# The last projection of a transformer pair in two token halves, from plain fp32 weights kept in the gather ring

## The chip, the cores and the metric

One core of a Trainium2 chip. The metric is the device time of one execution in microseconds, the median of the runs. Engines: TensorE (PE), VectorE (DVE), ScalarE (ACT), GpSimd (POOL), and SyncE (SP), which only issues DMAs here.

## What is computed

A two-layer transformer (feed-forward, gated linear attention, stick-breaking attention) is followed by one hybrid block. Only the end of that block matters here: 256 tokens, width 1024, fp32.

```python
mixed = sigmoid(g_s) * y_s + sigmoid(g_m) * (y_mlstm @ w_ml_out)
h = h + mixed @ w_out                        # the last projection
xn = rmsnorm(h, norm2_g)
q = (xn @ w_q).reshape(T, 8, 2, 128)         # 8 heads, two halves each
s = einsum('thid,hikd->thik', q, keys)       # 128 sub-keys for each half
sv, si = top_k(s, 16)                        # then the 16 best of 16 x 16 sums
gate = softmax(cs)                           # over the 16 experts chosen, ids eidx
act = gelu(einsum('td,thkd->thk', xn, u_tab[eidx]))
h = h + einsum('thk,thkd->td', gate * act, v_tab[eidx])
return rmsnorm(h, final_norm_g)
```

Each token reads 8 x 16 rows of a table that holds a row of `u` and one of `v` side by side (2048 fp32). With the tokens in two halves of 128 (one token per partition) that makes 2 x 8 x 16 = 256 gathers, each of 128 rows of 8 KB, 1 MiB.

## The kernel before

**Weights.** All weights but the last come as 512 KB packets (128 x 1024 fp32) that SyncE loads in order into six raw slots (`weights_in`, L511). ScalarE copies a packet to the high part (`refill`, L216), GpSimd subtracts it for the low part (L553), and TensorE multiplies high and low parts as fp32r. The sixteen packets of the query weights `w_q` are used as they came, in plain fp32: six in the raw slots, eight over the split buffers, one over `h`, and the last again in a raw slot (`query_slot`, L161; L534 to L542).

**The last two projections.** `mix_out` (L2305) multiplies `w_ml_out` (eight packets) and combines each of the eight 128-wide output chunks with the gates in PSUM (`total`, L2365), then splits the sums into `xs` (L2353, L2374). `add_projection` (L872) multiplies the eight packets of `w_out` for all 256 tokens: for each of eight chunks `mm_both` issues two matmuls, L208 (128x512: high weights by both parts of the input) and L209 (128x256). VectorE adds the residual (L927, L929), ScalarE copies the sum to `x` (L897) and writes it times the norm's gain to `over_xs` (L905).

**`peer` (L2389).** The first two query packets run for tokens 0 to 127 (`half(n, 0)`, L2565), then their key scores (`half_scores(0)`, L2572); VectorE's `first_route` (L2744) takes the best expert of head 0 at once and the next seven a little later, so that the first eight gathers can start. TensorE meanwhile runs the tokens 128 to 255 of the same packets, the sums of squares (`columns_pe`, L402), the transposes of the first half (`turn`, L2591), packets 2 and 3 for all tokens (`tile`, L2553) with their scores (L2583), and `begin(0)`, which puts the residual into the accumulators (L2598, L2600).

Then come 256 slots in order, one for each gather (n = 0 to 255; first half first; 16 per head):

- GpSimd issues gather n (L2659) into `ring[n % 8]`. For n of 8 or more it waits for `px_free`, the end of slot n - 8 on TensorE. Only eight gathers can be under way.
- VectorE multiplies and sums the `u` part with the token's hidden vector (`dot`, L2794) and between dots runs two steps of the routing of the next head.
- ScalarE makes gelu (L2474), weight (L2478) and a diagonal matrix (L2482), four of which exist.
- TensorE adds diagonal by `v` part in two 128x512 matmuls (L2608).

The other twelve query packets are put between slots by a table written out by hand, `PE_TILE_AT` (L47): a `tile` ahead of slots 2, 8, 16, 23 and so on up to 82, and the scores five slots behind every second one. The rings: six slots in the arena, one over `small_all`, one over `k.sq`; gather 7, into the last, waits for the norm's columns and for `pr_sqdone` (L2654).

The engines' queues are in order, so what stands ahead of slot 0 on TensorE or ScalarE delays it.

Of the kernel before, what the change touches and what calls it, by code (L numbers as in the profile page):

```python
# [15 lines left out]
P = 128  # L16
# [31 lines left out]
PE_EVICT_LAG = 3  # L48
PE_SCORES_LAG = 5
# [166 lines left out]
def refill(k, act, n, i=None):  # L216
# [3 lines left out]
    if i is None:  # L220
        if m >= AT["peer_q"]:
# [289 lines left out]
def weights_in(k, block, wstream):  # L511
# [3 lines left out]
    def _(sp):  # L515
# [8 lines left out]
        p0, last = AT["peer_q"], AT["peer_q"] + RAW  # L524
        full = last // RAW
# [6 lines left out]
        for n in range(full * RAW, last):  # L532
            sp.wait_ge(k.lo_done, n - RAW + 1)
            sp.dma_start(k.raw[:, n % RAW, :], wstream[n]).then_inc(k.landed[n % RAW], 16)  # L534
        for j in range(2 * SPLIT):

            if j % 2 == 0:
                sp.wait_ge(k.tile_done, p0 - SPLIT + j // 2 + 1)
            sp.dma_start(query_slot(k, RAW + j), wstream[last + j]).then_inc(k.query_in[j], 16)
        sp.dma_start(query_slot(k, 14), wstream[p0 + 14]).then_inc(k.query_in[8], 16)  # L540
        sp.wait_ge(k.tile_done, p0 + 1)
        sp.dma_start(query_slot(k, 15), wstream[p0 + 15]).then_inc(k.query_in[9], 16)  # L542
# [1762 lines left out]
def mix_out(k, block, ins):  # L2305
# [3 lines left out]
    sums, frees = k.mixes, k.frees  # L2309
    k.mixes += DC  # L2310
    k.frees += DC - 1
    late = 5
# [3 lines left out]
    def _(pe):  # L2316
# [22 lines left out]
        for n in range(3, 8):  # L2339
            wait_packet(k, pe, packet + n)  # L2340
            mm_packet(k, pe, packet + n, ps[:, bank[n], 0:SEQ], leaves=k.xs_free if n == 7 else None).then_inc(k.tile_done, 1)

    @block.scalar
    def _(act):
# [3 lines left out]
        def high(c):  # L2348

            if c < DC - 1:  # L2350
                act.wait_ge(k.xs_free, frees + c + 1)
            act.wait_ge(k.mix_sum, c + 1)
            act.activation(k.xs[:, 0, c, 0:SEQ], ps[:, bank[c], 0:SEQ], ACT.Copy).then_inc(k.mix_high, 1)  # L2353

        for n in range(6):
            refill(k, act, packet + n)
        for c in range(7):
            high(c)
        refill(k, act, packet + 6)
        high(7)  # L2360
        refill(k, act, packet + 7)

    @block.vector
    def _(dve):
        def total(n):  # L2365
            dve.wait_ge(k.tile_done, packet + n + 1)
            b = ps[:, bank[n], 0:SEQ]
            k.dve(dve.tensor_tensor(b, b, k.sig[:, 16 + n, :], ALU.mult))
            k.dve.settle(dve)
            dve.tensor_tensor(b, b, k.sig[:, 8 + n, :], ALU.add).then_inc(k.mix_sum, 1)  # L2370

        def rest(c):
            dve.wait_ge(k.mix_high, c + 1)
            dve.tensor_tensor(k.xs[:, 1, c, 0:SEQ], ps[:, bank[c], 0:SEQ], k.xs[:, 0, c, 0:SEQ].bitcast(F32), ALU.subtract  # L2374
                              ).then_inc(k.mix_ready, 1)

        dve.wait_ge(k.sig_made, 3)
        for n in range(7):
            total(n)
        for c in range(late):  # L2380
            rest(c)
        total(7)
        for c in range(late, DC):
            rest(c)

    add_projection(k, block, AT["w_out"], k.mix_ready, k.mixes, tuple(range(DC)), GAIN["norm2"], by_chunk=True, first=5, whole=True)


def peer(k, block, gain, ins, out):  # L2389
# [5 lines left out]
    k.norms += 1  # L2395
    k.early += 1
    k.columns += 1
# [34 lines left out]

    @block.scalar
    def _(act):
        late_refill(k, act)
        act.wait_ge(k.x_copied, k.copies)

        def square(i):
            act.activation(k.sq[:, 2 * i:2 * i + 2, 0:SEQ] if i else sum_bank(k, 7), x[:, 2 * i:2 * i + 2, :], ACT.Square
                           ).then_inc(k.sq_ready, 1)  # L2440

        def half(n, t):

# [664 lines left out]
```

## Time and profile before

| | |
|---|---|
| median of 3 runs | 1936.19 us (1935.8 to 1937.76) |
| the profiled execution's own time | 1936.39 us |
| its span, first to last instruction | 1934.6 us |
| mean granted TensorE clock | 0.995 |
| HBM read over the span | 484.10 MB |
| software-descriptor DMA queue (the gathers) | 268.45 MB, 36864 packets |
| first query product starts, `w_out` done | 1265.14 us |
| first slot's matmul starts | 1287.20 us |

How to read it: the page divides the span into 40 slices of 48 us; the gathers fill the last third. The timeline lists instructions of one engine in order, like ones merged, each with its start, its duration, and in brackets how long the engine had been idle and what released it. A plain fp32 matmul leaves two records (x2), an fp32r one leaves one.

### The profile page before, as it was taken

The page shows a single profiled execution, that of the slowest core. Times are in us where ns is not written, and L with a number is a line of the kernel's source. Part 1 is how long each engine was busy: PE and PEld are TensorE (multiplying, and loading weights), DVE is VectorE, ACT ScalarE, POOL GpSimd, SP SyncE. Part 2 cuts the span into 40 slices and gives each one's busy share as a digit, 9 for nine tenths or more (in the row PEclk, how much of TensorE's full clock was granted, in tenths as well). Part 3 has the DMA queues.
Part 4 walks back from the last instruction along what each step waited for, and adds up shares of the span by engine and source line. Part 5 has one row for each costly group of instructions (what it writes and reads, how often), then busy time and mean ns, then how long its engine had stood idle before and what let it go on. Part 6 is the DMA issues. An engine that isn't in the chain of part 4 may idle for free.

```text
span 1934.6 us, 29255 instructions
## 1 busy us (share of the span) xinstructions
PE 1804.0 (93%) x9861; PEld 1366.0 (71%) x9864; DVE 1145.7 (59%) x2481; ACT 949.7 (49%) x1757; POOL 1224.1 (63%) x708
## 2 busy tenths in 40 slices
PE   8999999999999999999999999999999877778777
PEld 7999888999999998789998878875544322222222
DVE  5444555444644466754457775576677666777664
ACT  5444646444544465654448445454444444444443
POOL 8888665888788877388887962534444343433441
PEclk9999999999999999999999999999999999999999
DMA  7666443666566555266654341599999999999996
GB/s 269 186 186 190 152 144 125 197 189 185 169 196 188 185 167 166 80 188 188 187 184 140 122 152 55 154 389 421 421 421 421 421 421 418 421 422 419 422 420 283
DMA packets 98426, 486.76 MB, mean 252 GB/s; under 512 B 11920, under 2 KB 12944, under 8 KB 65312
## 3 DMA queue, kind: packets, MB, share of 16 engines
q1 hardware_dynamic: 60304, 213.20, 35.6%
q0 software_dynamic: 36864, 268.45, 33.4%
q10 hardware_dynamic: 1168, 3.96, 0.6%
q8 instruction: 50, 0.82, 0.2%
q14 instruction: 40, 0.33, 0.0%
HBM read 484.10 MB, written 1.05 MB: 251 GB/s over the span
## 4 chain that ended last, share of the span: by engine, by line
PE 68%; DMA 16%; DVE 5%; ACT 5%; POOL 4%; issue 2%; DVEq 0%; ACTq 0%; POOLq 0%
DMA arena<-uv_tab,arena 16%; PE ps L827 16%; PE ps L2608 10%; PE ps L178 8%; PE ps L179 8%; PE ps L180 8%; PE ps L825 7%; PE ps L208 2%; POOL split L1824 2%; PE ps L2553 2%; DVE arena L2794 1%; ACT arena L2482 1%; PE ps L209 1%; PE ps L830 1%; POOL arena L1828 1%
## 5 line engine op out<-in xcount | busy, mean ns | idle before, releaser
L553 POOL TENSOR_TENSOR split<-raw,split 128x1024 fp32r<-128x1024 f32 x358 | 859.0, 2407 | 292.6 <-ACT split L228 287.9
L228 ACT ACTIVATE split<-raw 128x1024 fp32r<-128x1024 f32 x382 | 404.7, 1063 | 494.7 <-PE ps L180 263.0
L2608 PE MATMUL ps<-arena 128*128 128x512 f32 x1024 | 494.2, 617 | 101.7 <-ACT arena L2482 101.4
L2659 POOL DMA_INDIRECT arena<-uv_tab,arena x256 | 268.4, 1049 | 383.8 <-PE ps L2608 350.9
L827 PE MATMUL ps<-xs,split 128*128 128x512 f32 x1344 | 470.6, 393 | 0.0
L2608 PEld LDWEIGHTS ps<-arena 128*128 128x128 f32 x1024 | 181.9, 191 | 400.6 <-ACT arena L2482 248.2
L825 PE MATMUL ps<-xs,split 128*128 128x256 f32 x1176 | 328.5, 279 | 0.0
L827 PEld LDWEIGHTS ps<-xs,split 128*128 128x128 f32 x1344 | 247.0, 188 | 43.5
L825 PEld LDWEIGHTS ps<-xs,split 128*128 128x128 f32 x1176 | 221.1, 188 | 6.9
L2794 DVE CUSTOM_DVE_ANT_0 arena<-arena,raw 128x1024 f32<-128x1024 f32 x128 | 156.8, 1225 | 103.9 <-DMA arena<-uv_tab,arena 103.2
L2794 DVE CUSTOM_DVE_ANT_0 arena<-arena 128x1024 f32<-128x1024 f32 x128 | 156.9, 1226 | 91.4 <-DMA arena<-uv_tab,arena 90.6
L783 DVE TENSOR_TENSOR ps<-ps,arena 128x512 f32<-128x512 f32 x84 | 58.7, 699 | 250.4 <-PE ps L827 250.4
L2474 ACT ACTIVATE arena<-arena 128x1 f32<-128x1 f32 x256 | 51.8, 202 | 310.9 <-DVE arena L2794 310.7
L178 PE MATMUL ps<-h,split 128*128 128x256 f32 x704 | 199.0, 283 | 0.1
L180 PE MATMUL ps<-h,split 128*128 128x256 f32 x704 | 199.0, 283 | 0.0
L179 PE MATMUL ps<-h,split 128*128 128x256 f32 x704 | 198.9, 282 | 0.0
L178 PE MATMUL ps<-xs,split 128*128 128x256 f32 (+1 forms) x608 | 175.7, 289 | 4.4 <-POOL split L1824 2.8
L179 PE MATMUL ps<-xs,split 128*128 128x256 f32 (+1 forms) x608 | 172.2, 283 | 0.0
L180 PE MATMUL ps<-xs,split 128*128 128x256 f32 (+1 forms) x608 | 172.0, 283 | 0.0
L179 PEld LDWEIGHTS ps<-h,split 128*128 128x128 f32 x704 | 134.5, 191 | 3.4
L178 PEld LDWEIGHTS ps<-h,split 128*128 128x128 f32 x704 | 134.2, 191 | 0.4 <-issue 0.4
L180 PEld LDWEIGHTS ps<-h,split 128*128 128x128 f32 x704 | 134.4, 191 | 0.0
(424 smaller groups left out, 2742.2 us busy)
## 6 DMA issues: line engine op xcount, KB each, us to landing
raw<-wstream SPq DMA_DIRECT2D x393, 512.0 KB, 3.5
over_split<-wstream SPq DMA_DIRECT2D x8, 512.0 KB, 6.6
arena<-uv_tab,arena POOLq DMA_INDIRECT x256, 15.1
arena<-small SPq DMA_DIRECT2D x1, 1195.0 KB
arena<-xT SPq DMA_DIRECT2D x1, 1024.0 KB, 6.2
arena<-keys ACTq DMA_DIRECT2D x1, 1024.0 KB, 7.9
arena<-rows ACTq DMA_DIRECT2D x1, 512.0 KB, 4.5
over_h<-wstream SPq DMA_DIRECT2D x1, 512.0 KB, 8.4
```

The lines of the kernel that those rows point to most:

```text
L178: pe.matmul(out, w_hi, x_hi, start=start, stop=False, **kw)
L179: pe.matmul(out, w_hi, x_lo, start=False, stop=False, **kw)
L180: return pe.matmul(out, w_lo, x_hi, start=False, stop=stop, **kw)
L228: act.activation(parts_of(k, m)[0], raw_slot(k, m), ACT.Copy).then_inc(k.hi_done, 1)
L553: pool.tensor_tensor(lo, raw_slot(k, n), hi.bitcast(F32), ALU.subtract).then_inc(k.lo_done, 1)
L783: dve.tensor_tensor(both(4 + b), both(4 + b), rstd, ALU.mult).then_inc(k.gate_scaled, 1)
L825: pe.matmul(k.ps[:, bank, 0:SEQ], lo[:, c, :], k.xs[:, 0, c, 0:SEQ], start=False, stop=False, skip_group_check=True)
L827: last = pe.matmul(both(bank), hi[:, c, :], k.xs[:, :, c, 0:SEQ], start=(c == 0), stop=(c == DC - 1), skip_group_check=True)
L2474: k.act(act.activation(acts[:, b, s:s + 1], dots[:, b, s:s + 1], ACT.Gelu_apprx_tanh))
L2608: last = pe.matmul(ps[:, banks[t][0] + i, :], diag[:, n % 4, :], ring[n % NS][:, D + i * 512:D + (i + 1) * 512], start=False, stop=ends, s ...
L2659: pool.indirect_dma_start(ring[n % NS], None, ins["uv_tab"], bass.IndirectOffsetOnAxis(ap=ids[:, b, s:s + 1], axis=0)).then_inc(k.px_in[n ...
L2794: dve.tensor_tensor_reduce(u, u, ht[t], 1.0, 0.0, ALU.mult, ALU.add, dots[:, b, s:s + 1]).then_inc(k.px_dot, 1)
```

## The change

The last projection leaves `add_projection`. The mixed sums stay in `sig` as plain fp32 and aren't split. The eight packets of `w_out` are loaded unsplit into an arena range, `w_last`, over which four of the eight ring slots lie (ring numbers 4 to 7); a ring slot there may be gathered into once two of the packets are done with. Each packet is multiplied in plain fp32 for tokens 0 to 127 first (`last_part(n, 0)`); the products for tokens 128 to 255 (`last_part(n, 1)`) are put among the first tokens' query products, scores and transposes. The query products of packets 0 to 3 now all run in token halves, the second half only after `begin(0)`. The norm's column for the second half is made at slots 14 to 20. The query packets are loaded eight packets earlier, and packet 15 goes over the low half of `xs`. Gather 7 no longer waits for the norm; gathers 4 to 7 wait for second-half products 2, 4, 6 and 8.

```diff
+PE_NORM_AT = 18
 def weights_in(k, block, wstream):
...
-        for n in range(full * RAW, last):
-            sp.wait_ge(k.lo_done, n - RAW + 1)
-            sp.dma_start(k.raw[:, n % RAW, :], wstream[n]).then_inc(k.landed[n % RAW], 16)
+        sp.wait_ge(k.mix_ready, 3 * DC)
+        for j in range(DC):
+            sp.dma_start(k.w_last[:, j, :], wstream[w0 + j]).then_inc(k.last_in[j // 2], 16)
+        sp.dma_start(query_slot(k, 14), wstream[p0 + 14]).then_inc(k.query_in[4], 16)
+        for n in range(RAW):
+            sp.wait_ge(k.lo_done, w0 + n - RAW + 1)
+            sp.dma_start(query_slot(k, n), wstream[p0 + n]).then_inc(k.landed[n % RAW], 16)
         for j in range(2 * SPLIT):
             if j % 2 == 0:
-                sp.wait_ge(k.tile_done, p0 - SPLIT + j // 2 + 1)
+                sp.wait_ge(k.tile_done, w0 - SPLIT + j // 2 + 1)
...
 def mix_out(k, block, ins):
+        def total(n, lo=0, hi=SEQ):
+            b, s = ps[:, bank[n], lo:hi], k.sig[:, 8 + n, lo:hi]
+            k.dve(dve.tensor_tensor(b, b, k.sig[:, 16 + n, lo:hi], ALU.mult))
+            k.dve.settle(dve)
+            dve.tensor_tensor(s, b, s, ALU.add).then_inc(k.mix_ready, 1)
...
-    add_projection(k, block, AT["w_out"], k.mix_ready, k.mixes, tuple(range(DC)), GAIN["norm2"], by_chunk=True, first=5, whole=True)
 def peer(k, block, gain, ins, out):
...
+        def last_part(n, t, lo=0, hi=DC):
+            if t == 0 and lo == 0:
+                pe.wait_ge(k.last_in[n // 2], 32)
+                if n >= 2:
+                    pe.wait_ge(k.dve_emptied, emptied + n - 1)
+            if t and n % 4 == 0:
+                pe.wait_ge(k.dve_emptied, emptied + DC - 1 + n // 4)
             for c in range(lo, hi):
+                if n < 2 and t == 0:
+                    pe.wait_ge(k.mix_ready, sums + max(c, 5) + 1)
+                if n == 0 and t == 1 and c == DC - 1:
+                    pe.wait_ge(k.mix_ready, sums + DC + 1)
+                last = pe.matmul(area(n, t), k.w_last[:, n, c * P:(c + 1) * P], mixed[:, c, T[t]],
                                  start=(c == 0), stop=(c == DC - 1))
...
+        for n in range(2, DC):
+            last_part(n, 0)
         half(0, 0)
         half(1, 0)
-        half(0, 1, 0, 2)
-        pe.wait_ge(k.pr_q, 2)
+        last_part(0, 1)
         pe.wait_ge(k.keys_in, 16)
-        half_scores(0)
-        half(0, 1, 2, DC)
-        half(1, 1)
-        pe.wait_ge(k.sq_sum, r + 1)
-        columns_pe(k, pe, cq)
-        tiles.wait_emptied(pe, 1)
-        pe.wait_ge(k.pr_sc, 1)
-        half_scores(1)
+        half_scores(0, 0)
+        turn(0, 6)
+        half(2, 0)
+        half(3, 0)
+        last_part(1, 1)
+        columns(0)
+        last_part(2, 1)
         pe.wait_ge(k.col_rms, cq + 1)
-        turn(0, 6)
-        for n in range(2, PE_TILES_FIRST):
-            tile(n)
-            if n % 2:
-                scores(n // 2)
+        half_scores(1, 0)
+        for n in range(3, DC):
+            last_part(n, 1)
         pe.wait_ge(k.pr_ht, 1)
         begin(0)
+        half(0, 1)
+        half(1, 1)
+        half_scores(0, 1)
+        half(2, 1)
+        half(3, 1)
+        half_scores(1, 1)
         for n in range(SLOTS):
+            if n == PE_NORM_AT + 1:
+                pe.wait_ge(k.pr_sc, 6)
+                columns(1)
...
-            if n == NS - 1:
-                pool.wait_ge(k.col_rms, cq + 1)
-                pool.wait_ge(k.pr_sqdone, 1)
+            if NS // 2 <= n < NS:
+                pool.wait_ge(k.tile_done, w0 + 2 * (n - NS // 2) + 2)
...
+        def added(n, t):
+            dve.wait_ge(*((k.tile_done, w0 + (n | 3) + 1) if t else (k.last_half, n + 1)))
+            dve.tensor_tensor(x[:, n, T[t]], area(n, t), x[:, n, T[t]], ALU.add).then_inc(k.dve_emptied, 1)
...
         hidden(0, 6)
...
+        for n in range(DC):
+            added(n, 1)
         for g in range(GROUPS):
...
                 dot(g * PE_K + s)
+                if g * PE_K + s == PE_NORM_AT:
+                    squares(1, 1, 4)
+                if g * PE_K + s == PE_NORM_AT + 2:
+                    inverse(1)
```

ScalarE ahead of slot 0 now runs, in this order: `scaled(0, c)` (gain times x into `over_xs`) with three of the four squares, `half(0, 0)`, `half(1, 0)`, `half_scores(0, 0)`, the last square, the Sqrt table, `columns(0)`, `half(2, 0)`, `half(3, 0)`, `half_scores(1, 0)`, the first exponentials, `scaled(1, c)`, and the four halves and two scores of the second half. At slots 14 to 17 it runs `square(1, i)` and at slot 20 `columns(1)`.

## Rows read from the trace of the kernel before

**Rows 1.** The page, part 2: DMA throughput in 40 equal slices.

```profile
GB/s 269 186 186 190 152 144 125 197 189 185 169 196 188 185 167 166 80 188 188 187 184 140 122 152 55 154 389 421 421 421 421 421 421 418 421 422 419 422 420 283
```

**Rows 2.** Windows: us, busy of each engine, PEclk, DMA share, GB/s.

```profile
1220.00:1240.00 20.00, 19.46 (x165) 19.25 (x164) 9.58 (x22) 8.13 (x10) 11.60 (x5) 1.00 0.55 166
...
1260.00:1280.00 20.00, 20.00 (x141) 18.59 (x140) 12.33 (x52) 10.05 (x24) 4.33 (x5) 1.00 0.98 374
1280.00:1300.00 20.00, 18.61 (x75) 12.20 (x75) 19.31 (x58) 12.27 (x31) 8.78 (x9) 1.00 1.01 415
```

**Rows 3.** Timeline of VectorE, end of the mLSTM: start, us, operation.

```profile
1225.50 0.69 DVE L2132 TENSOR_TENSOR xs<-ps,xs 128x512 fp32r<-128x512 f32 x1 [0.74 <-ACT xs L1992]
```

**Rows 4.** Timeline of TensorE, first matmul of the projection.

```profile
1242.70 0.50 PE L208 MATMUL ps<-xs,split 128*128 128x512 f32 x1
```

**Rows 5.** Timeline of TensorE from the projection to the slots.

```profile
1265.14 4.38 PE L2565 MATMUL ps<-over_xs,raw 128*128 128x128 f32 x36
1269.44 0.71 PE L2572 MATMUL ps<-arena 128*128 128x128 f32 x4
1269.99 3.29 PE L2565 MATMUL ps<-over_xs,raw 128*128 128x128 f32 x28
1273.11 1.01 PE L402 MATMUL ps<-arena 128*128 128x1 f32 x8
...
1274.52 1.06 PE L2591 MATMUL ps<-arena 128*128 128x128 f32 x8
1275.41 7.07 PE L2553 MATMUL ps<-over_xs,raw 128*128 128x256 f32 x32
...
1284.38 1.95 PE L2600 MATMUL ps<-arena 128*128 128x128 f32 x16
1287.20 3.70 PE L2608 MATMUL ps<-arena 128*128 128x512 f32 x8 [0.87 <-ACT arena L2482]
1290.74 3.62 PE L2553 MATMUL ps<-over_xs,raw 128*128 128x256 f32 x16
1294.19 10.60 PE L2608 MATMUL ps<-arena 128*128 128x512 f32 x24
```

**Rows 6.** Timeline of ScalarE ahead of slot 0.

```profile
1284.15 0.66 ACT L2461 ACTIVATE arena<-ps 128x256 f32<-128x256 f32 x2 [1.25 <-PE ps L2583]
1284.83 1.28 ACT L2474 ACT_TABLE_LOAD   x1
...
1286.74 0.40 ACT L2482 ACTIVATE arena<-arena 128x128 f32<-128x128 f32 x1
```

**Rows 7.** Timeline of GpSimd: issues of gathers 0, 1, 8, 10, 16.

```profile
1272.70 1.15 POOL L2659 DMA_INDIRECT arena<-uv_tab,arena  x1 [14.57 <-DVE arena L2766]
1275.91 0.94 POOL L2659 DMA_INDIRECT arena<-uv_tab,arena  x1 [2.06 <-DVE arena L2716]
...
1289.96 0.94 POOL L2659 DMA_INDIRECT arena<-uv_tab,arena  x1 [4.48 <-PE ps L2608]
...
1296.34 0.94 POOL L2659 DMA_INDIRECT arena<-uv_tab,arena  x1 [3.96 <-PE ps L2608]
...
1310.73 1.91 POOL L2659 DMA_INDIRECT arena<-uv_tab,arena  x1 [4.19 <-PE ps L2608]
```

**Rows 8.** Tile view of one gather issue, number 1.

```profile
L2659 POOL DMA_INDIRECT arena<-uv_tab,arena x1: 939/939/939, 1275.9 to 1275.9; - x1
...
DMA to landing us min/median/max: 5.7/5.7/5.7
```

**Rows 9.** Timeline of VectorE: hidden vector; dots of slots 10, 16, 255.

```profile
1281.92 1.28 DVE L2673 SCALAR_TENSOR_TENSOR arena<-ps,arena 128x1024 f32<-128x1024 f32 x1
...
1305.74 1.23 DVE L2794 CUSTOM_DVE_ANT_0 arena<-arena 128x1024 f32<-128x1024 f32 x1 [0.91 <-DMA arena<-uv_tab,arena]
...
1320.54 1.23 DVE L2794 CUSTOM_DVE_ANT_0 arena<-arena 128x1024 f32<-128x1024 f32 x1 [1.25 <-DMA arena<-uv_tab,arena]
...
1924.71 1.23 DVE L2794 CUSTOM_DVE_ANT_0 arena<-arena,raw 128x1024 f32<-128x1024 f32 x1 [1.24 <-DMA arena<-uv_tab,arena]
```

More of the change, by code:

```diff
@@ L523, in _ @@
             sp.dma_start(dst, src).then_inc(k.small_in, 16)
-        p0, last = AT["peer_q"], AT["peer_q"] + RAW
-        full = last // RAW
+        w0, p0 = AT["w_out"], AT["peer_q"]
+        full = w0 // RAW
+        assert w0 % RAW == 0
         with sp.Fori(1, full) as i:
@@ L2308, in mix_out @@
     ps = k.ps
[L2309 to L2312, printed above, removed]
+    sums = k.mixes
+    k.mixes += DC + 1
     bank = (4, 2, 3, 5, 0, 1, 6, 7)
@@ L2346, in _ @@
         act.dma_start(k.peer_keys, ins["keys"]).then_inc(k.keys_in, 16)
[L2348 to L2355, printed above, removed]
[L2356 to L2361 removed]
+        for n in range(DC):
+            refill(k, act, packet + n)
     @block.vector
     def _(dve):
[L2365 to L2386 removed]
+        def total(n, lo=0, hi=SEQ):
[3 more added lines that the diff above has]
+            dve.tensor_tensor(s, b, s, ALU.add).then_inc(k.mix_ready, 1)
+        dve.wait_ge(k.sig_made, 3)
+        for n in range(DC):
+            dve.wait_ge(k.tile_done, packet + n + 1)
+            if n < DC - 1:
+                total(n)
+            else:
+                total(n, 0, P)
+                total(n, P, SEQ)
 def peer(k, block, gain, ins, out):
@@ L2394, in peer @@
     r, e0, cq = k.norms, k.early, k.columns
-    k.norms += 1
-    k.early += 1
-    k.columns += 1
+    w0 = AT["w_out"]
+    mixed = k.sig[:, DC:2 * DC, :]
+    sums, emptied = k.mixes - DC - 1, k.dve_tiles
+    T = (slice(0, P), slice(P, SEQ))
+    area = lambda n, t: ps[:, 2 + n // 4, P * (n % 4):P * (n % 4 + 1)] if t else ps[:, 2 + n % 2, 0:P]
     take = k.arena.take
@@ L2566, in half @@
                                  start=(c == 0), stop=(c == DC - 1))
             if hi == DC:
-                last.then_inc(k.tile_done if t else k.pr_half, 1)
-        def half_scores(t):
+                last.then_inc(k.tile_done if t else k.last_half, 1)
+        def half(n, t):
+            if t == 0:
+                query_landed(k, pe, n)
+            w = query_slot(k, n).rearrange("p (c m) -> p c m", c=DC)
+            for c in range(DC):
+                if n == 0:
+                    pe.wait_ge(k.xl_ready, DC * (e0 + t) + c + 1)
+                last = pe.matmul(half_at(n, t), w[:, c, :], k.over_xs[:, 0, c, T[t]], start=(c == 0), stop=(c == DC - 1))
+            last.then_inc(k.tile_done if t else k.pr_half, 1)
@@ L2573, in half_scores, with columns @@
                                  start=True, stop=True)
             last.then_inc(k.pr_s if t else k.pr_s0, 1)
+        def columns(t):
+            pe.wait_ge(k.sq_sum, r + t + 1)
+            for c in range(2):
+                last = pe.matmul(ps[:, 5 - t, 0:1], sq[:, c, :], k.ones[:, 0:1], start=(c == 0), stop=(c == 1))
+            last.then_inc(k.col_ss, 1)
         def scores(h):
             tiles.wait_emptied(pe, 2 * h + 1)
-            if h >= 2:
-                pe.wait_ge(k.pr_sc, 2 * (h - 1))
+            pe.wait_ge(k.pr_sc, max(2 * (h - 1), 4))
+            if h == 4:
+                pe.wait_ge(k.col_rms, cq + 2)
@@ L2664, in _, with squares @@
     def _(dve):
-        norm_low(k, dve, e0, x, gain)
-        sum_squares(k, dve, r, last=3)
+        def added(n, t):
+            dve.wait_ge(*((k.tile_done, w0 + (n | 3) + 1) if t else (k.last_half, n + 1)))
+            dve.tensor_tensor(x[:, n, T[t]], area(n, t), x[:, n, T[t]], ALU.add).then_inc(k.dve_emptied, 1)
+        def squares(t, first, last):
+            for i in range(first, last):
+                dve.wait_ge(k.sq_ready, 4 * (r + t) + i + 1)
+                step = dve.tensor_tensor(sq[:, 0:2, :], sq[:, 0:2, :], sq[:, 2 * i:2 * i + 2, :], ALU.add)
+                if i < 3:
+                    k.dve(step)
+                    k.dve.settle(dve)
+                else:
+                    step.then_inc(k.sq_sum, 1)
+        for n in range(DC):
+            added(n, 0)
+        squares(0, 1, 3)
         def hidden(t, first):
@@ L2815, in _ @@
             run(step)
+        for n in range(DC):
+            added(n, 1)
         for g in range(GROUPS):
```

157 lines of the change are left out of this document (93 added, 64 removed).

## The prediction

> **What bounds the kernel now.** I read the page's slices first. From the slice that begins near 1300 us to the last but one the DMA engines move 418 to 422 GB/s [rows 1]: the last third is a stream of 256 gathers of 1 MiB at the engines' full rate. The timeline of VectorE says the same: the dots of slots 10, 16 and 255 are released by their gather's landing [rows 9], and from dot 10 to dot 255 lie 618.97 us, 2.53 us for each. After dot 255 come a fixed 9.9 us to the end of the span. So the end is set by when the stream first runs without a gap, and the reader should ask of every edit: does gather 10 or 16 land earlier or later?
>
> What holds the stream's start? Gather 0 goes out at 1272.70 and the next from 1275.91 [rows 7], after the projection (1242.70 to 1265.14 [rows 4, 5]), two query packets and the scores. Gather 8 and later ones need a free ring slot, so they hang on TensorE's slots: slot 0 starts at 1287.20 and gather 8 goes out at 1289.96. TensorE is busy for 20.00 and 18.61 of 20 us in the two windows around this [rows 2]; it, and not the DMA, is the scarce engine there. The granted clock is 1.00 in all three windows [rows 2], that is 2.4 GHz.
>
> **How much slack the stream has.** Gather 1, issued to almost empty queues, landed 5.7 us after its issue [rows 8]. Gather 10 landed (dot 10 released) at 1305.74, 9.4 us after its issue at 1296.34; gather 16 9.8 us after its issue [rows 7, 9]. So issues may slip by 3.7 and 4.1 us before any landing does. Beyond that each microsecond is lost at the end.
>
> **Loads.** SyncE's eight packets of `w_out` go out when the mLSTM's last product is split, 1226.2 [rows 3], and the query packets behind them. The DMA share was 0.55 in 1220 to 1240 [rows 2], so there is room. Up to 1242.7 only the first two of them are needed; the eight are 4.2 MB, 10 us at 421 GB/s [rows 1], behind 1.5 MB of keys and gain on ScalarE's queue. I cost them at nothing; the 16 us of cover to 1242.7 hides them. SyncE's new wait stands ahead of the query packets, the first of which is wanted only after the first half of the projection; those loads are 8.4 MB, 20 us, and leave the time of the first gathers. ScalarE's sixteen copies and GpSimd's eight subtractions for `w_out` go, from engines that were not the bound.
>
> **Removed from TensorE.** The projection: 22.44 us, 1242.70 to 1265.14. VectorE's and ScalarE's splits of the mixed sums lay beside products; nothing for them.
>
> **Added to TensorE.** A plain fp32 product of 128 by 128 by 128: from 1269.99 to 1273.11 run 14 of them (28 records), 0.223 us each [rows 5]. The projection is now 128 of these. First half: 64, 14.3 us. Packet 2 waits for VectorE to empty packet 0's bank, because packets 0 and 1 end together; a 128-column add with its semaphores: below nothing is excluded, above I bound it by the 0.71 us of rows 5's score group, and take 0.4. So the first half ends at 1257.4 instead of 1265.14. The VectorE adds and ScalarE `scaled` of the last chunk must be through within the 1.6 us that chunks 0 to 6 of the next packet take, and cost nothing.
>
> **First gather.** Sixteen products (3.6), eight of the second half put in for cover (1.8), the scores (0.7): the scores end at 1263.4, against 1270.15 before (1269.44 + 0.71). All that follows on VectorE is as before, so gathers 0 and 1 are issued 6.7 us earlier, 1266.0 and 1269.2. Gathers 4 to 7 wait for second-half packets. From 1262.8 TensorE has two pairs of scores (1.1), the transposes (0.9), sixteen query products (3.6), the column (0.4) and 56 products of the second half (12.5), so the last is done near 1281.3, in time for gather 7's turn. By 2.5 us each, gather 7 lands near 1290 (1269.2 + 5.7 + 6 x 2.5).
>
> **Slot 0.** TensorE has, from 1242.7: 128 products of the projection (28.5), 64 of query packets 0 to 3 in halves (14.3), four pairs of scores at 0.55 (2.2; 1269.44 to 1269.99), the transposes (0.9, 1274.52 to 1275.41), one column (0.4; both took the 0.9 from 1273.11 to 1273.99), `begin(0)` (2.1, 1.95 of it L2600) [rows 5]: 48.4. Waits: 0.4 as above; two exposed evictions, since the scores of a second half stand right behind the product whose eviction by ScalarE they need, 0.6 each (the eviction takes 0.3, semaphores the rest; between 0.3 and 0.9); and the chain on ScalarE between the last scores and slot 0. Before, `begin(0)` covered that chain: ScalarE began on the scores at 1284.15, loaded the table at 1284.83, and slot 0 started at 1287.20 [rows 5, 6], 3.05 us, of which TensorE stood idle for 0.87. Now nothing lies behind the last scores. One eviction instead of two, so 2.8 us, all idle. Waits 4.4, sum 52.8: slot 0 starts at 1295.5, **8.3 us later** than now. VectorE's hidden vector, at 1281.92 now [rows 9] and near 1277 then (6.7 earlier, less some 1.7 of waiting for the column), and the eight adds of the second half (the last behind the last product, 1281.3, through by 1282.5) stay ahead of TensorE, which reaches the second half's query products at 1283. If that cover went, each would add its excess in full.
>
> **The stream.** Slots and tiles then follow as before (1.77 us a slot; 3.45 us for the tile ahead of slot 2 [rows 5]), so gather 8 goes out at 1298.3 and gather 10 at 1304.6. Gather 7 landed near 1290 and gather 8 lands at 1304.0: some 11 us in which the DMA engines have nothing to fetch. Gather 10 lands at 1304.6 + 5.7 = 1310.3, 4.6 us later than now. Gather 16, issued at 1319.0, would land at 1324.7, but the stream has it at 1310.3 + 14.8 = 1325.1: the lost time is 4.6 us and doesn't grow, since TensorE's slots at 1.77 us run ahead of 2.5 us again. The squares and the column at slots 14 to 20 with two table loads (1.28 each, rows 6) take some 3 us on ScalarE, but it is four diagonals ahead of TensorE there. Nothing. Sum: 8.3 - 3.7 = **+4.6 us**.
>
> The trace gives 5.7 us from issue to landing. The Trainium skill (DMA: Bandwidth & Descriptors, Anatomy of one DMA, SWDGE path) fits 2.0 us plus the bytes over 436 GB/s, 4.4 us for this gather. By that figure the stream's slack would be 5.0 us and the sum 3.3; I go by the row, since gather 1 is the same transfer from the same queue, and the page's fit may leave out part of GpSimd's 0.94 us.
>
> **Bounds.** Slack: 3.7, or 4.1 by gather 16. Waits on TensorE: 3.5 to 5.0. Gathers 1 to 7 now may take longer than 2.5 us, which changes only how long the DMA engines idle. If the stream after the pause starts less smoothly (a slot's issue 0.94 to 1.91 us on GpSimd [rows 7]), up to 2 us more. So the likeliest case runs from +3.0 to +7.
>
> **Rivals.** (1) *The early start decides* (faster). The first gathers go out 6.7 us earlier; if the stream then ran on without a gap, all landings would move by that, to 1929.7. It needs gather 8 out by 1286.8 (1290 + 2.5 - 5.7), so slot 0 at 1284, or that the second half's 14.3 us fill idle time of TensorE. Point from which it decides: no gain and no loss at slot 0 = 1290.8 (3.6 us later than now), a gain below it. Against: TensorE had only 1.4 us idle in 1260 to 1300 [rows 2], and the second half stands ahead of slot 0 in its queue. For: gathers were indeed the stream's bound, and 6.3 MB of query loads leave their way. (2) *Hardly anything* (same): the pause is shorter than I say since a gather to idle engines lands in 4.5 to 5.2 us and the evictions hide; +2 to +3.8. (3) *A second gap* (slower than forecast): the slots start 8 us late with 11 tiles still to be put between them; if gather 16 or 24 misses its time too, the cost goes to the full 8.3 us, 1944.7. For: gather 16 has only 0.4 us in hand. Against: from there it gains 0.7 us with every slot that has no tile.
>
> **How the numbers follow.** The profiled execution took 1936.39 us, its span 1934.6; 1936.39 + 4.6 = **1941.0 us**, 4.8 above the median of 1936.19, which the profiled time matches within 0.2. That is 0.25%; what a measurement of this kernel can tell from no change is about 0.2%, 3.9 us, so that the forecast sits just beyond it and part of its own spread falls inside. Chances: my forecast 0.50, rival 3 0.08, rival 2 0.22, rival 1 0.20 (in whole, or in part where the load on DMA or TensorE differs from my reading). A quarter of the forecast's own half lies under 3.9 us by its bounds, and of rival 1 little is within 0.2%: slower 0.50, same 0.31, faster 0.19. The range, 1934.0 to 1945.0, holds the forecast, rivals 2 and 3, and the weak part of rival 1.
>
> **What the changed profile would show.** Right: first-half products end near 1257.4; gather 0 near 1266; a dip of DMA throughput in the slices or windows from about 1288 to 1300; slot 0 on TensorE near 1295.5 with TensorE idle 2 to 3 us before it; gather 8 issued near 1298; dot 10 near 1310; 9.9 us from the last dot to the end. Wrong: slot 0 before 1291, or dots 3 to 12 at an even 2.5 us with no pause. A late `last_in` would show as idle time of TensorE at 1242.7, a full VectorE as `xl_ready` waits near 1283; either would make it slower than said.

## The result and the profile after

The changed kernel takes **1944.72 us** (median of 6 runs, 1944.22 to 1946.44), the kernel before 1936.32 us (median of 6, 1935.80 to 1937.76). The ratio is 1.0044, 95% interval 1.0031 to 1.0057: 8.4 us slower. The forecast was 1941.0 us in a range of 1934 to 1945; the side was right, the size was put at 4.6 us. The profiled execution shown here took 1946.44 us (span 1944.7), 1.7 us above the median.

The page's throughput in slices, which answers to [rows 1]:

```profile
GB/s 267 187 187 187 152 152 127 197 185 185 172 194 186 188 170 160 85 189 188 184 173 140 140 119 44 292 253 413 421 421 421 421 420 409 421 421 422 409 413 296
```

The last third is again a stream at the full rate, and after the last dot nothing has changed (VectorE: 1934.74 to the end at 1944.7, 9.9 us as before). Slice 27, 253 instead of 389, is where the gathers' start lies. Windows of that stretch (us, busy of each engine, PEclk, DMA share, GB/s), answering to [rows 2]:

```profile
1260.00:1280.00 20.00, 20.00 (x181) 19.95 (x180) 12.62 (x57) 6.17 (x15) 6.77 (x7) 1.00 0.69 259
1280.00:1300.00 20.00, 16.46 (x98) 12.65 (x96) 18.17 (x53) 8.49 (x26) 1.87 (x2) 0.83 0.41 172
...
1288.00:1290.00 2.00, 2.00 (x21) 2.00 (x20) 1.93 (x7) 0.28 (x1) 0.00 (x0) 1.00 0.15 53
...
1292.00:1294.00 2.00, 0.00 (x0) 0.00 (x0) 1.97 (x7) 1.86 (x4) 0.00 (x0) 0.77 0.00 0
1294.00:1296.00 2.00, 1.65 (x2) 0.84 (x3) 1.93 (x5) 1.87 (x8) 0.00 (x0) 0.50 0.00 0
1296.00:1298.00 2.00, 2.00 (x4) 0.74 (x3) 1.97 (x4) 1.19 (x6) 0.00 (x0) 0.50 0.00 0
1298.00:1300.00 2.00, 2.00 (x4) 0.94 (x3) 0.69 (x2) 0.40 (x1) 0.94 (x1) 0.52 0.00 0
...
1324.00:1326.00 2.00, 2.00 (x7) 0.81 (x5) 1.23 (x2) 0.00 (x0) 1.22 (x2) 1.00 0.85 303
```

Three things are to be seen. The DMA engines have nothing to do from 1290 to 1300 (the pause that was forecast). TensorE does nothing in 1292 to 1294, and behind that its clock is 0.50 (1.2 GHz) instead of 1.00 until 1300 (which wasn't forecast). And DMA dips once more at 1324 to 1326.

TensorE's timeline from the projection to the slots (start, us, operation, idle before and its releaser), answering to [rows 4, 5]; L2584 is the projection, L2597 a half query packet, L2650 the slots:

```profile
1241.43 3.73 PE L2584 MATMUL ps<-arena 128*128 128x128 f32 x32
1245.42 10.96 PE L2584 MATMUL ps<-arena 128*128 128x128 f32 x96 [0.25 <-DVE arena L2720]
1256.21 3.74 PE L2597 MATMUL ps<-over_xs,raw 128*128 128x128 f32 x32
...
1270.93 9.10 PE L2584 MATMUL ps<-arena 128*128 128x128 f32 x80
...
1280.30 1.95 PE L2642 MATMUL ps<-arena 128*128 128x128 f32 x16
1282.08 3.74 PE L2597 MATMUL ps<-over_xs,raw 128*128 128x128 f32 x32
1286.18 0.71 PE L2607 MATMUL ps<-arena 128*128 128x128 f32 x4 [0.36 <-ACT arena L2453]
1286.73 3.74 PE L2597 MATMUL ps<-over_xs,raw 128*128 128x128 f32 x32
1290.83 0.71 PE L2607 MATMUL ps<-arena 128*128 128x128 f32 x4 [0.37 <-ACT arena L2453]
1294.35 6.44 PE L2650 MATMUL ps<-arena 128*128 128x512 f32 x8 [2.81 <-ACT arena L2493]
1300.63 3.62 PE L2567 MATMUL ps<-over_xs,raw 128*128 128x256 f32 x16
1304.09 10.46 PE L2650 MATMUL ps<-arena 128*128 128x512 f32 x24
```

The projection starts at 1241.43 here and at 1242.70 in the trace before. That start lies between 1241.35 and 1244.50 in the thirteen profiles of this study, in no order, so from here on I count from it and write it +. Slot 0 stands at +52.92, before at +44.50. The four products of slots 0 and 1 (eight records) last from 1294.35 to the tile at 1300.63, 6.28 us; before, 1287.20 to 1290.74, 3.54 us [rows 5]. That is the clock's fall: 2.74 us in this trace. It varies: in a_late, behind the same idle time, they take 5.20 us, 1.66 more.

GpSimd's issues of gathers 0, 1, 7, 8, 10 and 16, answering to [rows 7]:

```profile
1264.73 1.15 POOL L2711 DMA_INDIRECT arena<-uv_tab,arena  x1 [28.09 <-DVE arena L2834]
1267.74 0.94 POOL L2711 DMA_INDIRECT arena<-uv_tab,arena  x1 [1.87 <-DVE arena L2784]
...
1280.30 0.94 POOL L2711 DMA_INDIRECT arena<-uv_tab,arena  x1 [2.64 <-PE ps L2584]
1298.92 0.94 POOL L2711 DMA_INDIRECT arena<-uv_tab,arena  x1 [17.68 <-PE ps L2650]
...
1306.24 0.94 POOL L2711 DMA_INDIRECT arena<-uv_tab,arena  x1 [4.24 <-PE ps L2650]
...
1320.50 1.29 POOL L2711 DMA_INDIRECT arena<-uv_tab,arena  x1 [4.32 <-PE ps L2650]
```

And VectorE's dots 8, 10, 11, 12, 15, 16 and 255, answering to [rows 9]:

```profile
1304.52 1.23 DVE L2867 CUSTOM_DVE_ANT_0 arena<-arena 128x1024 f32<-128x1024 f32 x1 [5.80 <-DMA arena<-uv_tab,arena]
...
1311.71 1.23 DVE L2867 CUSTOM_DVE_ANT_0 arena<-arena 128x1024 f32<-128x1024 f32 x1 [2.64 <-DMA arena<-uv_tab,arena]
...
1314.14 1.23 DVE L2867 CUSTOM_DVE_ANT_0 arena<-arena 128x1024 f32<-128x1024 f32 x1 [1.20 <-DMA arena<-uv_tab,arena]
...
1317.22 1.23 DVE L2867 CUSTOM_DVE_ANT_0 arena<-arena 128x1024 f32<-128x1024 f32 x1 [1.84 <-DMA arena<-uv_tab,arena]
...
1324.71 1.22 DVE L2867 CUSTOM_DVE_ANT_0 arena<-arena 128x1024 f32<-128x1024 f32 x1 [1.24 <-DMA arena<-uv_tab,arena]
...
1328.74 1.22 DVE L2867 CUSTOM_DVE_ANT_0 arena<-arena 128x1024 f32<-128x1024 f32 x1 [2.79 <-DMA arena<-uv_tab,arena]
...
1934.74 1.23 DVE L2867 CUSTOM_DVE_ANT_0 arena<-arena,raw 128x1024 f32<-128x1024 f32 x1 [1.24 <-DMA arena<-uv_tab,arena]
```

Dot 10 to dot 16 takes 17.03 us, before 14.80. The largest step is dot 15 to 16, 4.03 us, beside the dip at 1324. The tile ahead of slot 8 (3.45 us) holds gather 16 back to 1320.50, when only gathers 14 and 15 are still on their way. That the tile makes this step isn't shown: a_drop issues gather 16 at the same +79.1 and has a step of 2.49 us there, a_tiles issues it 4.5 us earlier and has 3.76.

### The profile page after: what moved, and what is told of

Same layout as the page of the kernel before. It is cut to its first block, busy times and chain, and to the rows that moved or that the text cites. A ratio compares the mean times of both kernels' runs of the same rounds, so it can differ in the third digit from the quotient of the medians.

```text
span 1944.7 us, 29505 instructions
## 1 busy us (share of the span) xinstructions
PE 1813.3 (93%) x10024; PEld 1377.6 (71%) x10024; DVE 1140.9 (59%) x2479; ACT 941.0 (48%) x1750; POOL 1202.2 (62%) x700
## 4 chain that ended last, share of the span: by engine, by line
PE 69%; DMA 16%; DVE 5%; ACT 5%; POOL 4%; issue 1%; DVEq 0%; ACTq 0%; POOLq 0%
DMA arena<-uv_tab,arena 16%; PE ps L843 16%; PE ps L2650 10%; PE ps L191 8%; PE ps L193 8%; PE ps L192 8%; PE ps L841 7%; POOL split L1840 2%; DVE arena L2867 1%; PE ps L2584 1%; PE ps L221 1%; PE ps L2567 1%; ACT arena L2493 1%; PE ps L846 1%; POOL arena L1844 1%
## 5 line engine op out<-in xcount | busy, mean ns | idle before, releaser
L569 POOL TENSOR_TENSOR split<-raw,split 128x1024 fp32r<-128x1024 f32 x350 | 839.5, 2405 | 290.7 <-ACT split L241 285.8
L241 ACT ACTIVATE split<-raw 128x1024 fp32r<-128x1024 f32 x374 | 396.2, 1062 | 484.8 <-PE ps L193 258.0
L2650 PE MATMUL ps<-arena 128*128 128x512 f32 x1024 | 498.3, 622 | 102.3 <-ACT arena L2493 101.9
L2650 PEld LDWEIGHTS ps<-arena 128*128 128x128 f32 x1024 | 184.8, 194 | 402.2 <-ACT arena L2493 243.7
```

The lines of the kernel that those rows point to most:

```text
L241: act.activation(parts_of(k, m)[0], raw_slot(k, m), ACT.Copy).then_inc(k.hi_done, 1)
L569: pool.tensor_tensor(lo, raw_slot(k, n), hi.bitcast(F32), ALU.subtract).then_inc(k.lo_done, 1)
L2650: last = pe.matmul(ps[:, banks[t][0] + i, :], diag[:, n % 4, :], ring[n % NS][:, D + i * 512:D + (i + 1) * 512], start=False, stop=ends, s ...
```

## The experiments

Eleven kernels were run, each beside the kernel before on the same chip. This table holds them all; times in the middle are counted from the projection's first product, and the last column is the median minus that of the kernel before in the same set of runs.

| kernel | slot 0 | gather 10 issued | dot 10 | dot 16 | dot 28 | median us | minus before |
|---|---|---|---|---|---|---|---|
| before | 44.50 | 53.64 | 63.04 | 77.84 | 107.68 | 1936.32 | |
| after | 52.92 | 64.81 | 70.28 | 87.31 | 117.99 | 1944.72 | +8.4 |
| b_pad18 | 47.37 | 56.42 | 65.02 | 79.82 | 109.93 | 1937.33 | +0.5 |
| b_pad36 | 51.23 | 60.28 | 66.41 | 83.29 | 113.11 | 1941.48 | +4.6 |
| a_warm | 52.92 | 62.07 | 67.81 | 84.53 | 114.37 | 1942.60 | +5.7 |
| a_begin | 51.11 | 60.26 | 65.96 | 83.07 | 112.89 | 1941.03 | +4.2 |
| a_late | 52.92 | 63.73 | 69.98 | 86.86 | 116.70 | 1945.51 | +8.8 |
| a_drop | 52.93 | 64.88 | 70.40 | 86.77 | 117.29 | 1943.07 | +6.3 |
| a_defer | 42.62 | 51.77 | 60.41 | 75.41 | 105.37 | 1932.77 | -4.0 |
| a_defer49 | 42.63 | 48.68 | 60.48 | 75.57 | 105.36 | 1932.90 | -3.8 |
| a_tile11 | 52.92 | 64.97 | 70.37 | 86.98 | 119.27 | 1948.67 | +11.9 |
| a_tiles | 52.92 | 60.32 | 69.11 | 85.17 | 115.00 | 1943.94 | +7.2 |
| a_warmtiles | 52.92 | 58.61 | 67.72 | 82.89 | 112.70 | 1941.57 | +4.8 |

From dot 28 to dot 255 the profiles took 572.7 to 575.9 us, in no order (574.33 before, 575.32 after); a difference at dot 28 is therefore good to 1 or 2 us of the time, no better.

**The price of a late slot 0, on the kernel before.** Small bf16 products on a spare bank stand ahead of `begin(0)`; nothing else changes. The second kernel has 36 in place of 18.

```diff
+        keep_warm(k, pe, 18, bank=3)
         pe.wait_ge(k.pr_ht, 1)
         begin(0)
```

> The kernel before with 18 small bf16 matmuls (3.9 us at full clock) put on TensorE between the scores of head 1 and begin(0); they compute nothing that is used. Theory of the ring (the end moves only when slot 2 frees its ring slot more than 3.7 us late): 0.9 us of the 3.9 fill TensorE's idle time ahead of slot 0, slot 0 starts 3.0 us later, and the time stays within 1 us of before. Rival (every microsecond ahead of slot 0 is on the path): 3.0 us longer.

> The same with 36 such matmuls (7.8 us). Theory of the ring: slot 0 6.9 us later, of which 3.7 are slack, so 3 to 4 us longer than before. Rival (everything ahead of slot 0 counts): 6.9 us longer. Rival (the gathers' stream alone sets the end): no change.

Measured: 1937.33 us (ratio 1.0006, 0.9997 to 1.0015) and 1941.48 us (1.0029, 1.0017 to 1.0041). Slot 0 came 2.87 and 6.73 us later. The first costs nothing that the medians can tell, though its trace has dot 10 2.0 us late; the second costs 4.6 us, more than the 3 to 4 expected and less than the rival's 6.9. So a late slot 0 alone, with none of the change's other parts, costs the greater part of what was seen. By these times 2.1 to 2.4 us of lateness are free, not the 3.7 of the prediction: with 36 products gather 10 is issued 6.6 us late, dot 10 comes 3.4 us late, and dot 16 already 5.5.

**Only the clock.** On the changed kernel, twelve such products behind the last scores, to fill the idle 2.81 us.

```diff
         half_scores(1, 1)
+        keep_warm(k, pe, 12, bank=3)
         for n in range(SLOTS):
```

> The changed kernel with 12 small bf16 matmuls (2.6 us, result unused) in the 2.8 us in which TensorE waited ahead of slot 0. Theory that the fallen clock was part of the loss: granted clock 1.00 around slot 0, slots 0 and 1 in 3.5 us together in place of 6.4, and some 2.5 to 3 us of the 8.4 come back. Rival (the slots catch up anyway, the clock cost nothing at the end): within 1 us of the changed kernel.

Measured: 1942.60 us (1.0035, 1.0021 to 1.0049), 2.1 us back by the medians (2.7 by the table's last column; 2.5 to 3 were expected). TensorE's timeline, and then two windows (PEclk, DMA share and GB/s are the last three columns):

```profile
1292.13 2.54 PE L255 MATMUL ps<-zero_bf 128*128 128x512 bf16 x11
1294.89 3.70 PE L2650 MATMUL ps<-arena 128*128 128x512 f32 x8 [0.22 <-ACT arena L2493]
1298.43 3.62 PE L2567 MATMUL ps<-over_xs,raw 128*128 128x256 f32 x16
```

```profile
1294.00:1296.00 2.00, 1.78 (x7) 0.73 (x5) 1.90 (x7) 1.78 (x8) 0.00 (x0) 1.00 0.00 0
1296.00:1298.00 2.00, 2.00 (x7) 0.81 (x5) 1.97 (x4) 1.78 (x8) 0.34 (x1) 1.00 0.00 0
```

Slot 0 starts at the same +52.92, the clock stays at 1.00, slots 0 and 1 take 3.54 us again, and gather 10 goes out 2.74 us earlier. Nothing else was changed, so the clock is a term by itself.

**Cover for ScalarE's chain.** `begin(0)` moved behind the second half's scores, where it stood before the change.

```diff
-        pe.wait_ge(k.pr_ht, 1)
-        begin(0)
         half(0, 1)
...
         half_scores(1, 1)
+        pe.wait_ge(k.pr_ht, 1)
+        begin(0)
```

> The changed kernel with begin(0) moved behind the last scores ahead of slot 0, where it stood before the change. Theory: it covers 2.1 of the 2.8 us of waiting, and TensorE stays busy, so the clock stays up: slot 0 some 2.1 us earlier and slots 0 and 1 2.9 us shorter, together 4 to 5 us of the 8.4 back (1940 to 1941). Rival (only the clock mattered): 2.5 to 3 us. Rival (neither is on the path): no change.

Measured: 1941.03 us (1.0023, 1.0013 to 1.0034), 4.2 above before. Its TensorE timeline:

```profile
1290.41 1.95 PE L2642 MATMUL ps<-arena 128*128 128x128 f32 x16
1292.95 3.70 PE L2650 MATMUL ps<-arena 128*128 128x512 f32 x8 [0.60 <-ACT arena L2493]
1296.49 3.62 PE L2567 MATMUL ps<-over_xs,raw 128*128 128x256 f32 x16
```

Idle time ahead of slot 0 is 0.60 instead of 2.81 us, slot 0 is 1.81 us earlier and the clock doesn't fall. Half of the change's loss was this order alone, idle time and clock together, and the time met the expected 1940 to 1941.

**Are the early gathers worth anything?** Gather 1 and those behind it wait for tile 5 of the projection.

```diff
+            if n == 1:
+                pool.wait_ge(k.tile_done, w0 + 6)
```

> The changed kernel, with the second gather and those behind it held until tile 5 of the last projection is done, some 10 us later than now. Theory (slot 0 starts too late; the early start of the gathers is worth nothing, since the ring is full from 1281 us on and only a freed slot lets gather 8 go): within 1 us of the changed kernel, 1944 to 1946 us. Rival (the stream needs the data that it gathers ahead of the blocks): the dots slip with the gathers and the kernel takes 4 to 10 us more.

Measured: 1945.51 us (1.0047, 1.0031 to 1.0062), which is 0.8 us from the changed kernel in other runs. GpSimd issued gather 1 at 1278.20 instead of 1267.74, and gather 8 at 1299.72, as in the changed kernel (+57.3 and +57.5). Behind a slot 0 that comes this late, ten microseconds of early start are worth nothing, as the theory had it.

**Less work of TensorE ahead of slot 0.** 35 products of the second half are left out, so the output for tokens 128 to 255 lacks most of packets 3 to 7.

```diff
         def last_part(n, t, lo=0, hi=DC):
+            if t and n >= 3:
+                lo = DC - 1
```

> The changed kernel, with 35 of the products of the second token half of packets 3 to 7 left out (the output of tokens 128 to 255 lacks most of these parts of the last projection). That takes 35 x 0.223 = 7.8 us of TensorE's work away ahead of slot 0. Theory (the time is that of slot 0's start, through the release of gather 8): slot 0 at about 1286.5, 5 to 8 us back, 1937 to 1940 us. Rival (the loss is later, in the first blocks or in a shorter gather ring): under 2 us back, 1943 to 1945 us.

Measured: 1943.07 us (1.0031, 1.0018 to 1.0045). Slot 0 didn't move at all, which neither theory said. Its TensorE timeline shows why:

```profile
1271.10 1.28 PE L2586 MATMUL ps<-arena 128*128 128x128 f32 x10
1277.58 0.63 PE L2642 MATMUL ps<-zero_bf 128*128 128x512 bf16 x1 [5.21 <-DVE arena L2743]
1278.01 3.62 PE L2644 MATMUL ps<-arena 128*128 128x128 f32 x16
1281.42 4.56 PE L2599 MATMUL ps<-over_xs,raw 128*128 128x128 f32 x32
```

`begin(0)` waits 5.21 us for VectorE's hidden vector, and the clock is at 0.63 in 1275 to 1280 and 0.69 in 1280 to 1285, where `begin(0)`'s transposes take 3.62 instead of 1.95 us. The 7.8 us taken out come back as 5.2 us of waiting and 2.5 us of slower work (3.62 - 1.95 and 4.56 - 3.74). So the run doesn't test what it was made for, and shows something else: in the changed kernel the hidden vector is done at 1276.8 and TensorE reaches `begin(0)` at 1279.86, so of work taken out ahead of it no more than some 3 us could have come back. That slot 0 stands at just the same place is chance, waiting and slower work making up for the 7.8 us. Why its median is 1.6 us below the changed kernel's with slot 0 unmoved stays open; its dot 28 is 0.7 us earlier.

**The work moved behind slot 0.** The second tokens' query halves of packets 0 to 3 and their scores go to slots 42, 57, 72 and 86. They need room of their own for the queries (`qT2`, in a buffer free by then) and scores in other banks; the waits follow. The second version also puts the first two tiles ahead of slots 4 and 9 instead of 2 and 8.

```diff
+PE_HALF_AT = {42: 0, 57: 1, 72: 2, 86: 3}
+    qT2 = k.raw[:, 5, 0:4 * P].rearrange('p (n t) -> p n t', n=4)
...
         begin(0)
-        half(0, 1)
-        half(1, 1)
-        half_scores(0, 1)
-        half(2, 1)
-        half(3, 1)
-        half_scores(1, 1)
         for n in range(SLOTS):
...
+            if n in PE_HALF_AT:
+                half(PE_HALF_AT[n], 1)
+            m = PE_HALF_AT.get(n - PE_SCORES_LAG, 0)
+            if m % 2:
+                half_scores(m // 2, 1)
```

> The changed kernel, with the second-token query halves of the first four packets and their scores moved from ahead of slot 0 into slots 42 to 86 of the stream, where TensorE has idle time. Theory (start of slot 0 decides, and the stream is bound by DMA from gather 10 on): slot 0 at about 1284, gather 10 issued 3 to 4 us earlier than in the kernel before, and a time 3 to 6.7 us under it, 1930 to 1934 us. Rival (TensorE's work in the stream is not covered: what is moved comes back there): 1936 to 1944 us.

> As the one before, with the first two tiles of the stream's side work in slots 4 and 9 instead of 2 and 8, so that slots 2 and 3 free their buffers sooner. Theory: gather 10 is issued about 2 us earlier still, and the time is 0 to 2 us under that of the one before. Rival (the release of gather 8, not of gather 10, sets the stream): no difference over 0.7 us.

Measured: **1932.77 us** (11 runs, ratio 0.9981, 0.9972 to 0.9990), 4.0 us under the kernel before and some 12 under the changed kernel; and 1932.90 us (0.9978, 0.9969 to 0.9988). This version beats both kernels. TensorE's timeline of the first:

```profile
1280.93 1.95 PE L2648 MATMUL ps<-arena 128*128 128x128 f32 x16
1284.69 3.70 PE L2656 MATMUL ps<-arena 128*128 128x512 f32 x8 [1.81 <-ACT arena L2500]
1288.23 3.62 PE L2577 MATMUL ps<-over_xs,raw 128*128 128x256 f32 x16
```

Slot 0 starts at +42.62, 1.9 us before that of the kernel before, and the pause of the DMA engines is gone, though they don't reach the full 421 GB/s until 1320, as its windows show (DMA share and GB/s are the last two columns):

```profile
1280.00:1300.00 20.00, 17.43 (x65) 10.38 (x66) 18.77 (x54) 12.61 (x34) 8.29 (x7) 1.00 0.95 371
1300.00:1320.00 20.00, 20.00 (x62) 10.68 (x61) 12.09 (x28) 9.63 (x34) 9.64 (x10) 1.00 0.97 377
1320.00:1340.00 20.00, 17.60 (x52) 9.17 (x51) 18.01 (x48) 12.91 (x32) 9.60 (x8) 1.00 1.01 424
```

What was moved doesn't come back in the stream: from dot 28 to dot 255 this trace takes 573.37 us, which is in the spread of all. Of the 4.0 us its trace shows 2.3 at dot 28 (+105.37 against +107.68); the rest lies where single traces scatter, ahead of the projection and behind dot 28. How much of the gain is slot 0's start and how much the gathers' earlier start wasn't separated. The second version issues gather 10 3.1 us earlier still and gains nothing (dot 10 at +60.48 against +60.41): with the queues full, its rival holds.

**Where the tiles stand.** On the changed kernel, in the list of slots that a tile stands ahead of:

```diff
-(2, 8, 16, 23, 31, 38, 46, 53, 61, 68, 75, 82)
+(2, 11, 16, 23, 31, 38, 46, 53, 61, 68, 75, 82)   a_tile11
+(5, 10, 16, 23, 31, 38, 46, 53, 61, 68, 75, 82)   a_tiles; a_warmtiles, which has a_warm's line too
```

> The changed kernel, with the tile that stands ahead of slot 8 put ahead of slot 11. The changed kernel's dots 10 and 16 lie 17.03 us apart where the stream's pace makes it 14.9; the largest single step is from dot 15 to dot 16, 4.03 us instead of 2.49. Theory (the slack at gather 16 is used up by the tile ahead of slot 8): gather 16 is issued 3.5 us earlier, dots 15 and 16 lie 2.5 us apart, and up to 1.5 us come back, less what gather 19 loses in the same way: 1943 to 1944.5 us. Rival (the step belongs to the restart of the DMA queues, wherever the tile stands): the step stays, 1944.5 to 1946 us.

> The changed kernel, with the tiles ahead of slots 2 and 8 put ahead of slots 5 and 10. Slot 0 starts as in the changed kernel, and the clock falls as there. Theory (both tiles delay a gather that has no slack after the pause): gather 10 is issued near 1302.8 instead of 1306.2, dots 8 to 12 come every 2.5 us from 1304.5 on, and 2 to 4 us come back, 1941 to 1943 us. Rival (gather 8, that is slot 0's start, sets the stream whatever stands between): 1944 to 1946 us.

> The changed kernel with both edits: twelve small products that keep TensorE busy in the idle time ahead of slot 0, as in a_warm, and the tiles ahead of slots 5 and 10. If the clock's fall and the tiles' places are separate terms, their gains add: 2.1 us (a_warm) and what the run with the tiles alone gives back, 1938.5 to 1941 us. Rival (they are one term, since a slower slot 0 and a tile ahead of slot 2 delay the same gather, 10, and gather 8 is then the bound): no more than 1 us below the better one of the two.

Measured: 1948.67 us (1.0058, 1.0045 to 1.0072), 1943.94 us (1.0040, 1.0026 to 1.0053) and 1941.57 us (1.0026, 1.0017 to 1.0036). The first is a miss of another kind. Gather 16 was issued 3.3 us earlier and the step from dot 15 to 16 shrank from 4.03 to 2.97 us, but then VectorE stood still:

```profile
1328.83 1.23 DVE L2867 CUSTOM_DVE_ANT_0 arena<-arena 128x1024 f32<-128x1024 f32 x1 [1.74 <-DMA arena<-uv_tab,arena]
...
1337.12 0.49 DVE L2756 MAX8 arena<-arena 128x8 f32<-128x128 f32 x2 [7.06 <-ACT arena L2468]
```

The top-k of the second tokens needs the tile's scores between dots 16 and 17, and with the tile three slots later they are 7.06 us late. The place of a tile is bound from both sides. With both tiles moved, dots 9 to 12 come 2.5 us apart as expected, but dot 8 to 9 takes 3.7, and only 0.8 us come back by the medians against 2 to 4 expected; dots 15 to 16 take 3.76 there, though gather 16 was issued 10.6 us ahead of its dot. Both kernels with two tiles moved show a_tile11's wait too, 2.49 and 3.08 us between dots 16 and 17, but dots 16 to 28 take 29.8 us as before, so it costs nothing. With the clock's fall filled as well, dots 10 and 16 lie 15.17 us apart (changed kernel: 17.03), and the time is 1.0 us below a_warm's and 2.4 below a_tiles'. That is the sum of the two measured gains (2.1 and 0.8), a little over the expected 1938.5 to 1941, but also the edge of what the rival allowed, 1 us below the better one. The times alone don't decide between them.

## Why the prediction was right in its direction and 4 us short

Point by point, times from the projection's first product.

**Sum for slot 0.** Forecast 52.8 us, measured 52.92. The first half of the projection took 14.8 us (forecast 14.7, its wait 0.25 instead of 0.4), a half packet the forecast rate, the exposed evictions 0.36 and 0.37 us of idle time instead of 0.6 each, the idle time ahead of slot 0 2.81 against 2.8. The waits are 0.6 us less than said (3.8 against 4.4) and the work 0.7 more (49.1 against 48.4), so that the last tenths agree by luck. First-half products ended at +14.8 (14.7), gather 0 went out at 1264.73 (+23.3, forecast +23.3), VectorE's hidden vector at 1275.55 (+34.1; forecast near 1277, +34.3). That the early gathers buy nothing is shown by a_late. **Right.**

**"Slots and tiles then follow as before (1.77 us a slot)". Wrong.** The idle 2.81 us that the same text forecast brought the clock to 0.50 while slots 0 and 1 ran. The text had noted a clock of 1.00 in its three windows of before and taken it over. The same trace shows the fall further on, in the stream (TensorE's timeline, then one window):

```profile
1335.42 1.98 PE L2608 MATMUL ps<-arena 128*128 128x512 f32 x4 [0.30 <-ACT arena L2482]
1339.47 3.67 PE L2608 MATMUL ps<-arena 128*128 128x512 f32 x4 [2.07 <-ACT arena L2482]
```

```profile
1340.00:1342.00 2.00, 2.00 (x3) 0.67 (x2) 1.94 (x4) 0.44 (x2) 0.00 (x0) 0.50 1.02 426
```

Behind 2.07 us of idle time the same four records take 3.67 instead of 1.98 us, so the price could have been read before the run. Gather 10 went out 11.2 us later than before, not 8.3. a_warm puts this step at 2.74 us of issue and 2.1 us of time.

**Slack 3.7 us at gather 10. Right as to gather 10, wrong as to the stream.** Gather 10 landed 5.47 us after its issue (before: 9.40), so 3.9 us of slack were used. But the text gave gather 16 "4.1 us" and said of the lost time that it doesn't grow. Gather 16's issue-to-landing fell from 9.81 to 8.24 us only, not to 5.7, with gathers 14, 15 and 17 under way beside it. The loss at dot 10 is 7.2 us, at dot 16 9.5 us. That is rival 3, "a second gap", in part, but mostly not where it was looked for. From dot 10 to dot 16 the seven traces with a pause or deep dip of DMA and the tile ahead of slot 2 take 16.4 to 17.1 us, those without one (before, b_pad18, a_defer, a_defer49) 14.80, 14.80, 15.00 and 15.09. Only in the trace shown here is dot 15 to 16 the largest of these steps. In the other six it is dot 10 to 11, 3.4 to 4.1 us, and in four of them gather 16 then lands 2.49 us behind gather 15, as in a full stream. In that stretch the engines move less than the 421 GB/s of [rows 1]; two windows of a_warm (its dots 10 to 13 come between 1309.78 and 1319.03):

```profile
1304.00:1308.00 4.00, 4.00 (x11) 1.81 (x10) 1.63 (x5) 3.71 (x10) 2.70 (x3) 1.00 0.82 297
1308.00:1312.00 4.00, 4.00 (x11) 1.80 (x10) 1.88 (x6) 2.80 (x10) 3.02 (x3) 1.00 0.94 336
```

In a_tiles and a_warmtiles gathers 8 to 12 go out with no tile between them; dots 10 to 16 take 16.06 and 15.17 us, and a_warmtiles is 1.0 us below a_warm. That too few gathers under way are the reason for the slow restart is likely but not shown.

The sum with both: a_warmtiles, which has neither, is **4.8 us** above before, where 4.6 was forecast; the tiles' places add 1.0 and the clock 2.1, 7.9 in all, against 8.4 measured. The rest is within what the medians scatter. The term that was mis-sized beside the clock is thus the slack: of a slot 0 that is 8.4 us late a_warm, at the full clock, pays 5.7, so 2.7 us are free and not 3.7. That rival 3's own figure, 1944.7, is just what was measured is chance: it had no slack left and no fall of the clock.

The Trainium skill (DMA: Bandwidth & Descriptors, Anatomy of one DMA, SWDGE path), by which a gather is an estimated 4.4 us, is too short here in both cases: gather 10 took 5.47 us to nearly idle engines and gather 16 8.24 us. Going by the row was the better choice, and still too low for a restarted stream.

**Rival 1** (faster) fell in this form: slot 0 at +52.9 is far behind the turning point. But its condition, that the second half's query products go where TensorE is idle, is what a_defer does, and there it holds in part: slot 0 at +42.6 and 4.0 of its 6.7 us faster than before. **Rival 2** (hardly anything) fell: the pause was 10 us and none of gathers 8 to 10 landed in under 5.4 us. **Loads**, costed at nothing: TensorE waited for no load in this stretch, right.

## What to carry to other kernels

Work moved to start a stream early is worth nothing if the ring behind it must wait for an engine whose queue became longer: ask which buffer release the stream hangs on after its first round, and move work past that point, not ahead of it. An idle time that a prediction itself puts on TensorE must be priced twice, once as waiting and once as slower products behind it, by rows at both clocks. A latency read from a lone transfer was a lower bound here: for slack take the gathers that travel in company.

## What the runs showed of the hardware

**The clock falls on short idle times.** In the changed kernel TensorE had been busy for 49.1 of the 50.1 us before the 2.81 us of idle time, and the granted clock was at 0.50 from near 1293.1 (0.77 over 1292 to 1294) to 1300, some 7 us, 1.3 of them idle; in a_late, behind the same idle time, for some 3.5 us. 0.87, 0.60 and 1.81 us of idle time ahead of slot 0 (before, a_begin, a_defer) left it at 1.00; 2.81 (after, a_late, a_drop, a_tile11, a_tiles) and 5.21 us (a_drop) did not. In the stream, up to 1380 us, idle times of 1.53 (after), 1.59 (b_pad36) and 1.93 us (a_tile11) left it at 1.00, while 2.07 (before), 2.06 (b_pad18) and 2.25 us (a_tile11) did not. Small bf16 products in the idle time kept it at 1.00 and cost nothing themselves. The Trainium skill (TensorE: Matmul & The Clock Gate, The HAM clock gate) says that the clock is either full or half and that the engine's activity decides; the windows here, 1.00 and 0.50 with mixtures only where it changes, agree.

**A restarted gather queue is slower than its lone gather.** After a pause the first gather lands in 5.4 to 5.9 us (6.2 in a_late, whose pause was shorter), the second in 6.0 to 8.2 us, and with the tile ahead of slot 2 the dots come every 2.49 us again from dot 11 at the earliest. So a pause of the DMA engines costs more than the lateness of its first gather: 1.6 to 2.3 us more from dot 10 to dot 16.
